# Two transformer stacks on one core: who stores the experts' blocks, and in which order the work between the last two layers is issued

## Chip, core and metric

The program runs on one core of one Trainium2 chip. The core has five engines with queues of their own: PE (TensorE, matrix products), DVE (VectorE), ACT (ScalarE), POOL (GpSimd) and SP (SyncE, which here only issues transfers). They meet through semaphores: an instruction raises one, a wait on another engine holds that engine's queue until it has the value. The metric is the time of one execution on the device in microseconds, lower is better.

## What is computed

A first stack of two layers over 256 tokens (feed-forward, mixer, feed-forward, gated side input), then a second stack of two layers over the same 256 tokens and 256 tokens of context. The change lies in the second stack, in the first of its layers' mixture of experts and in the start of its second layer:

```python
for i in range(DEPTH):                       # DEPTH = 2
    h  = _modulate(_rmsnorm(x,  norm1_g[i]), sh1,  sc1)
    hc = _modulate(_rmsnorm(xc, norm1_g[i]), shc1, scc1)
    y, yc = mixer(h, hc)                     # layer 1: queries from h, keys and values from h and hc
    x = x + g1 * y                           # and xc alike, in layer 0
    h2 = _modulate(_rmsnorm(x, norm2_g[i]), sh2, sc2)
    f = _hier_moe(tokens, ...)               # tokens: h2, in layer 0 with the context's behind it
    x = x + g2 * f[:s]                       # and xc alike, in layer 0
return _rmsnorm(x, final_g)

def _hier_moe(t, ...):                       # 32 experts, two for each token
    xb = t_pad[buf_tok].reshape(n_blk, MOE_BLOCK, d)     # tokens sorted by expert, in blocks
    yb = (silu(x_blk @ w_gate[e]) * (x_blk @ w_up[e])) @ w_down[e]
    out.at[buf_tok].add(yb * buf_w)          # each token: its two experts' rows, weighted
```

## The kernel before

**Layout.** All activations of the second stack lie in SBUF (one tensor, `arena`), features on the 128 partitions: `k.x` is 8 feature tiles by 512 tokens, tokens 0 to 255 being x and 256 to 511 the context. Four token tiles of 128 follow from this: t = 0 and 1 are x's, t = 2 and 3 the context's. Products go to PSUM (`ps`). Everything is float32.

**Experts of layer 0** (`pe_experts_picked` and its counterparts, lines 2254 to 2360). A block is 32 assigned rows of one expert. How many blocks an expert has is known on the chip alone, so each engine runs, for each of 32 experts, a loop whose bounds it reads from SBUF (`first_block`). For a block, PE makes gate and up (line 2274, 64 products of 128 columns by four row groups, 128 records in the trace), picks the next block's rows (line 2249), turns the hidden values (line 2281) and the next rows (line 2575) and makes down (line 2289). ACT applies silu (line 2304) and copies the next block's rows out (line 2306). DVE makes the hidden product (line 2343), copies both turned tiles (2346, 2325) and prepares the pick of the block after (2237 to 2243). The down product of 32 rows lies on the partitions as four groups of 32, each with a quarter of the 1024 columns; ACT copies it to a ring of two places, `yring` (line 2309).

**Stores.** ACT stores too. In the loop over block g, `act_store_rows` (lines 2313 to 2319) stands between the copy of line 2306 and that of line 2309: it waits for the copy of block g - 1 and **for the stores of block g - 2 to have landed** (semaphore `y_out`), and then issues four transfers of 32 rows by 256 columns with the result of block g - 1 into the DRAM tensor `expert_out`. After the last expert it is called once more for the last block.

**Weights.** SP loads 6 MB an expert as three transfers of 2 MB (line 1890), into ten places of 2 MB, nine of them used here. The loads of expert e are issued once expert e - 3 has ended (`moe_ended`, raised by line 2292). PE waits for gate and up before an expert's loop, for down in the first block.

**Between the layers.** When the last expert has ended, GpSimd waits for all stores, raises `pool_ended` (line 2357) and issues eight indirect gathers of 512 KB (line 2360), two for each of the four token tiles. For each tile ACT scales one gathered tile (2368), DVE adds the other (2377), PE turns eight 128 by 128 squares (2395), DVE adds them to `k.x` (2383). When all four tiles are done, ACT squares the eight feature tiles of all 512 tokens (1376), PE sums them with a matrix of ones (1369), ACT takes the root (1385), DVE the reciprocal (1403), then DVE and ACT make the normed tiles, 8 features by two streams (1408, 1390). PE makes eight query tiles q1 of x (line 1443, eight products each, 16 records in the trace) and after each the rotation of the one before (1425), then the keys (k1) of both streams. In ACT's queue six small loads for layer 1 stand behind the normed tiles (`b_sink`, router weights, a table of constants). SP loads the second layer's query, key and value weights in four chunks (8 to 11) once experts 30 and 31 have ended, and the output weights (12 and 13) right behind.

**Layer 1** has its own experts' stage, with the results added in PSUM and no stores. Its weights come through ten places of 2 MB, each reloaded when its last reader has ended.

## Time and profile before

| | us |
|---|---|
| median of 3 runs | 3054.65 |
| lowest and highest run | 3050.98 and 3055.48 |
| profiled execution | 3052.24 |
| its span, first to last instruction | 3050.9 |
| PE busy (share of the span) | 2681.6 (88%) |
| DVE, ACT, GpSimd busy | 750.2, 481.6, 103.3 |
| experts of layer 0, first product to last result | 1799.6 to 2305.4 |
| from there to the first query product | to 2360.2 |
| query tiles, to the first key product | to 2394.3 |

A profile is of one execution, and its times of single steps are to be set against that execution's 3052.24 us. A row of a timeline gives start and duration and, in brackets, how long the engine stood idle before it and what ended the wait. DMA shares are means over 16 transfer engines; above 0.99 they have no gap. PEclk 1.00 stands for 2.4 GHz and 0.50 for 1.2 GHz.

### The profile page before, as it was taken

To read this page: it belongs to the slowest core of one execution; us is meant where nothing else is said; L and a number is where in the kernel's file an instruction comes from. 1 tells how busy PE (TensorE), PEld (TensorE's weight loads), DVE (VectorE), ACT (ScalarE), POOL (GpSimd) and SP (SyncE) were. 2 spreads that over 40 slices of the span, in tenths; PEclk is the share of its full clock that TensorE was granted. 3 is DMA by queue.
4 is the path that set the end of the run, shared out by engine and by line. 5 is a ranking of instruction groups with operands and counts; after the bars stand their busy time and mean duration, and the time that the engine had idled before them with its cause. 6 is when DMAs were issued, how large, how long until landed. Compare 5 with 4: busy or idle time off the path is not lost.

```text
span 3050.9 us, 57138 instructions
## 1 busy us (share of the span) xinstructions
PE 2681.6 (88%) x24486; PEld 1990.2 (65%) x24486; DVE 750.2 (25%) x2036; ACT 481.6 (16%) x1179; POOL 103.3 (3%) x144
## 2 busy tenths in 40 slices
PE   8999999999999999997997888887774998777766
PEld 7888688887888788884444556665552566554444
DVE  2002520023002520013117421111113153332223
ACT  2001310011001310012006320110002052000001
POOL 1001010011001010010000000000001000000000
PEclk9999999999999999998999999999986999999999
DMA  7544474546553466535210049899996114999997
GB/s 263 184 161 129 144 253 166 180 142 214 165 181 111 161 235 202 186 112 189 85 56 28 31 182 414 346 362 420 421 420 225 60 56 173 405 419 419 420 419 309
DMA packets 254651, 689.99 MB, mean 226 GB/s; under 512 B 15119, under 2 KB 148958, under 8 KB 238046
## 3 DMA queue, kind: packets, MB, share of 16 engines
q1 hardware_dynamic: 237696, 674.96, 58.6%
q10 hardware_dynamic: 15582, 7.61, 0.9%
q8 instruction: 173, 2.83, 0.4%
q0 software_dynamic: 1152, 4.19, 0.3%
q14 instruction: 48, 0.39, 0.0%
HBM read 669.95 MB, written 16.78 MB: 225 GB/s over the span
## 4 chain that ended last, share of the span: by engine, by line
PE 69%; DMA 17%; DVE 6%; issue 3%; ACT 3%; ACTq 2%; POOL 0%; SPq 0%; DVEq 0%
PE ps L663 18%; PE ps L674 10%; DMA arena<-in_moe_w_up 10%; DMA expert_out<-arena 7%; PE ps L1443 6%; PE ps L2607 3%; PE ps L1489 2%; PE ps L894 2%; PE ps L687 2%; PE ps L2274 2%; PE ps L1054 2%; PE ps L2030 2%; ACTq L2319 2%; PE ps L2568 1%; PE ps L2631 1%
## 5 line engine op out<-in xcount | busy, mean ns | idle before, releaser
L663 PE MATMUL ps<-arena 128*128 128x256 f32 x2560 | 568.6, 379 | 3.5 <-DVE arena L745 3.5
L663 PEld LDWEIGHTS ps<-arena 128*128 128x128 f32 x2560 | 483.0, 189 | 73.8 <-issue 4.1
L674 PE MATMUL ps<-arena 128*128 128x256 f32 x1408 | 318.0, 379 | 0.0
L674 PEld LDWEIGHTS ps<-arena 128*128 128x128 f32 x1408 | 264.9, 189 | 46.2 <-issue 8.4
L2274 PE MATMUL ps<-arena 128*32 128x128 f32 x6016 | 192.9, 286 | 55.3 <-issue 53.4
L2274 PEld LDWEIGHTS ps<-arena 128*32 128x32 f32 x6016 | 178.3, 115 | 64.2 <-issue 60.4
L2607 PE MATMUL ps<-arena 128*32 128x128 f32 x4096 | 139.8, 295 | 74.7 <-issue 72.9
L1443 PE MATMUL ps<-arena 128*128 128x512 f32 (+2 forms) x512 | 192.8, 548 | 11.3 <-ACT arena L1390 11.2
L787 DVE TENSOR_TENSOR arena<-arena,ps 128x256 f32<-128x256 f32 x76 | 32.1, 422 | 638.4 <-ACT arena L755 633.8
L2607 PEld LDWEIGHTS ps<-arena 128*32 128x32 f32 x4096 | 126.2, 119 | 82.6 <-issue 81.7
L1443 PEld LDWEIGHTS ps<-arena 128*128 128x128 f32 (+1 forms) x512 | 89.5, 180 | 104.7 <-issue 97.4
L755 ACT ACTIVATE arena<-ps 128x256 f32<-128x256 f32 x76 | 29.2, 384 | 675.1 <-PE ps L663 675.1
L2249 PE MATMUL ps<-arena 128*32 128x256 f32 x1536 | 102.4, 397 | 9.8 <-issue 6.8
L2289 PE MATMUL ps<-arena 128*32 128x256 f32 x1504 | 100.5, 406 | 4.1 <-issue 3.8
L2343 DVE TENSOR_TENSOR arena<-arena,ps 128x128 f32<-128x128 f32 x47 | 13.5, 288 | 360.0 <-ACT arena L2304 360.0
L2631 PE MATMUL ps<-arena 128*32 128x256 f32 x1024 | 63.8, 388 | 35.6 <-DVE arena L2719 35.6
L2249 PEld LDWEIGHTS ps<-arena 128*32 128x32 f32 x1536 | 58.9, 114 | 35.2 <-issue 11.8
L532 POOL TENSOR_TENSOR arena<-arena 128x256 f32<-128x256 f32 x64 | 42.8, 670 | 1081.4 <-DVE arena L500 1072.9
L894 PE MATMUL ps<-arena 128*128 128x256 f32 x352 | 77.4, 379 | 0.0
L2289 PEld LDWEIGHTS ps<-arena 128*32 128x32 f32 x1504 | 50.6, 114 | 38.1 <-issue 17.0
L2568 PE MATMUL ps<-arena 128*32 128x256 f32 x528 | 68.4, 638 | 8.0 <-issue 4.7
L894 PEld LDWEIGHTS ps<-arena 128*128 128x128 f32 x352 | 66.3, 189 | 9.5
(441 smaller groups left out, 2988.3 us busy)
## 6 DMA issues: line engine op xcount, KB each, us to landing
arena<-in_moe_w_gate SPq DMA_DIRECT2D x64, 2048.0 KB, 23.0
arena<-in_moe_w_up SPq DMA_DIRECT2D x64, 2048.0 KB, 24.7
arena<-in_moe_w_down SPq DMA_DIRECT2D x64, 2048.0 KB, 29.5
arena<-in_mod_w SPq DMA_DIRECT2D x24, 2048.0 KB, 13.2
arena<-in_w_gate SPq DMA_DIRECT2D x44, 1024.0 KB, 5.5
arena<-in_w_up SPq DMA_DIRECT2D x44, 1024.0 KB, 8.1
arena<-in_w_down SPq DMA_DIRECT2D x44, 1024.0 KB, 4.9
arena<-in_w_in SPq DMA_DIRECT2D x12, 1024.0 KB, 6.0
```

What stands on the lines that cost most here:

```text
L663: last = pe.matmul(k.ps[:, T % 4, off:off + S], w[:, t, T % 2 * P:(T % 2 + 1) * P], h[:, t, :], start=(t == 0), stop=(t == KT - 1), skip_g ...
L674: last = pe.matmul(acc[:, t, :], d[:, T % 2, t * P:(t + 1) * P], k.hid[:, T % 4, :], start=(T == 0 and t % 2 == 0), stop=end, skip_group_c ...
L687: last = pe.matmul(k.ps[:, T, off:off + S], w[:, t, T * P:(T + 1) * P], k.hu[:, t, :], start=(t == 0 and off == 0), stop=(t == KT - 1), sk ...
L894: last = pe.matmul(dst, w[:, t, j * P:(j + 1) * P], src[:, t, :], start=(t == 0), stop=(t == KT - 1), skip_group_check=True)
L1054: last = pe.matmul(k.banks(4, 4, S)[:, j, :], w[:, t, (j % 2) * P:(j % 2 + 1) * P], k.y[:, t, :], start=(t == 0), stop=(t == KT - 1), skip ...
L1443: last = pe.matmul(k.ps[o:o + m, j % 4, 0:ntok], w[:, t, c0:c0 + m], k.h2[:, t, 0:ntok], start=(t == 0), stop=(t == KT - 1), tile_position ...
L2249: last = k.nc.tensor.matmul(k.ps[32 * q:32 * q + 32, 1, 0:256], m.pick[:, t, :], m.rows[:, t, 256 * q:256 * q + 256], start=(t == 0), stop ...
L2274: last = pe.matmul(ps[BL * q:BL * q + BL, 0, a:a + F], m.xeT[:, t, :], wv[:, t, F * q:F * q + F], start=(t == 0), stop=(t == KT - 1), tile ...
L2289: last = pe.matmul(ps[BL * q:BL * q + BL, 3, 0:W], m.hT[:, f, :], wd[:, f, W * q:W * q + W], start=(f == 0), stop=(f == 3), tile_position= ...
L2568: last = k.nc.tensor.matmul(k.ps[32 * q:32 * q + 32, bank, 0:256], m.pick[:, t, :], rows, start=(t == 0), stop=(t == 1), tile_position=(0, ...
L2607: last = pe.matmul(ps[BL * q:BL * q + BL, 0, a:a + F], m.xeT[:, t, :], wv[:, t, F * q:F * q + F], start=(t == 0), stop=(t == KT - 1), tile ...
L2631: last = pe.matmul(ps[BL * q:BL * q + BL, 3, 0:W], m.hT[:, f, :], wd[:, f, W * q:W * q + W], start=(f == 0), stop=(f == 3), tile_position= ...
```

## The change

It has three parts.

1. GpSimd stores the blocks. ACT's four transfers a block are gone; `yring` has four places instead of two; ACT's copy of block g waits for `y_gone`, which GpSimd raises when it comes to a block whose parity's last stores have landed. GpSimd's loop takes two blocks a turn, one on semaphore `y_even`, one on `y_odd`. There are 47 blocks, so its last turn stores one place that holds no new block, and two pairs of stores ahead of the loop give both semaphores their first value. The gathers then wait for both.
2. Between the layers the two tiles of x are finished first, through norm and first query tile. The context's two tiles are combined, turned, added, summed and normed between the query tiles. The gathers land in `slots2[0]` and `Kflat`.
3. The six small loads of layer 1 are SP's. Chunk 11 waits for the gathers of tile 1, chunks 12 and 13 for the last turned context tile.

```diff
@@ act_experts_picked
             act.activation(m.xe, ps[:, 1, 0:256], ACT.Copy).then_inc(m.n["x_out"].sem, 1)
-            act_store_rows(k, m, g)
             act.wait_ge(*m.step("down", g, 1, 1))
-            act.activation(m.yring[:, bass.ds((g & 1) * W, W)], ps[:, 3, 0:W], ACT.Copy).then_inc(m.n["y_ready"].sem, 1)
-    act_store_rows(k, m, first_block(k, m, NE, ENG.Activation))
+            act.wait_ge(*m.step("y_gone", g, 0, 1))
+            act.activation(m.yring[:, bass.ds((g & 3) * W, W)], ps[:, 3, 0:W], ACT.Copy).then_inc(m.n["y_ready"].sem, 1)
+    act.activation(m.unread[:, 0:1], k.eps, ACT.Copy).then_inc(m.n["y_ready"].sem, 1)
@@ new, on GpSimd
+def pool_store_rows(k, m, g, b, which):
+    pool, BL, W = k.nc.gpsimd, m.BL, m.W
+    pool.wait_ge(*m.step("y_ready", b, 1, 1))
+    pool.wait_ge(which, g * STORE + STORE)
+    pool.wait_ge(m.n["y_gone"].sem, b + RING_AHEAD)
+    pool.tensor_tensor(m.unread[:, 1:2], m.unread[:, 2:3], m.unread[:, 2:3], ALU.add).then_inc(m.n["y_gone"].sem, 1)
+    pool_store(k, m, b, which)
+def pool_store(k, m, b, which):
+    for q in range(4):
+        k.nc.gpsimd.dma_start(k.ybuf[bass.ds(b * BL, BL), W * q:W * q + W], m.yring[BL * q:BL * q + BL, bass.ds((b & 3) * W, W)]).then_inc(which, 16)
@@ pool_experts
-    total = first_block(k, m, NE, ENG.Pool)
+    pairs = (first_block(k, m, NE, ENG.Pool) + 1) >> 1
+    pool_store(k, m, MAXROWS // m.BL + 2, even)
+    pool_store(k, m, MAXROWS // m.BL + 3, odd)
+    with pool.Fori(0, pairs) as g:
+        pool_store_rows(k, m, g, g * 2, even)
+        pool_store_rows(k, m, g, g * 2 + 1, odd)
+    pool.wait_ge(even, pairs * STORE + STORE)
+    pool.wait_ge(odd, pairs * STORE + STORE)
     pool.wait_ge(*s["moe_ended"].at(l, "expert", NE - 1))
-    pool.wait_ge(*m.step("y_out", total + 1, 0, 64))
@@ new, in place of pe_combine, pe_sums and pe_project for q1
+def pe_queries_between(k, m):
+    for t in range(2):
+        for g in range(2):
+            pe_turn_results(k, m, t, g, 2 * t + g)
+    for t in range(2):
+        for g in range(2):
+            pe_sum_part(k, t, g, 6 + t)
+    for j in range(KT):
...
+        last.then_inc(*s["pr_tile"].up("q1", j))
+        if j > 0:
+            pe_rotate_queries(k, j - 1)
+        if j == 1:
+            pe_turn_results(k, m, 2, 0, 6)
+            pe_turn_results(k, m, 2, 1, 7)
+        if j == 2:
+            for g in range(2):
+                pe.wait_ge(*s["moe_added"].at(0, 2, g))
+                pe_turn_results(k, m, 3, g, 6 + g)
+        if j == 4:
+            pe.wait_ge(*s["moe_added"].at(0, 3, 1))
+            for t in (2, 3):
+                for g in range(2):
+                    pe_sum_part(k, t, g, 4 + t)
+    pe_rotate_queries(k, KT - 1)
+def act_queries_between(k, m):
...
+    for j in range(KT):
+        act_project_tile(k, "q1", k.Q, S, j)
+        if j == 2:
+            for t in (2, 3):
+                for g in range(2):
+                    act_square_part(k, m, t, g)
...
+        if j >= 6:
+            for t in range(3 * j - 16, 3 * j - 13):
+                act_shift_stream(k, t, 1)
+def dve_queries_between(k, m):
...
+    dve_weigh(k, m, 0)
+    dve_weigh(k, m, 1)
+    for t in range(2):
+        for g in range(2):
+            dve_add_results(k, m, t, g, 2 * t + g)
...
+    for t in range(KT):
+        dve_norm_stream(k, t, 0)
+    dve_weigh(k, m, 2)
+    dve_weigh(k, m, 3)
+    for j in range(KT):
+        dve_project_tile(k, "q1", k.Q, S, j)
+        if j < 2:
+            for g in range(2):
+                dve_add_results(k, m, 2 + j, g, 6 + g)
...
+        if j >= 6:
+            for t in range(3 * j - 16, 3 * j - 13):
+                dve_norm_stream(k, t, 1)
@@ sp_program
-    sp_chunk(k, 11, 5, columns(w, D + S, S), s["moe_ended"].at(0, "expert", 31))
+    sp_chunk(k, 11, 5, columns(w, D + S, S), s["gathered1"].at(0, 1))
     w = a["b_w_o_2"][0]
-    sp_chunk(k, 12, 0, columns(w, 0))
+    sp_chunk(k, 12, 0, columns(w, 0), s["moe_turned"].at(0, 3, 1))
     sp_chunk(k, 13, 1, columns(w, 512))
+    sp.dma_start(k.sink, a["b_sink_2"].broadcast_to([P, 16])).then_inc(*s["sink_in"].up())
+    router_load(k, sp, ms[1])
+    sp.dma_start(*ms[1].const3).then_inc(*s["const31"].up(1))
```

The parts named in the new functions are the old steps cut by token tile: `act_weigh` and `dve_weigh` combine one tile of 128 tokens, `pe_turn_results` turns four squares, `dve_add_results` adds four, `act_square_part` and `pe_sum_part` take four feature tiles of 128 tokens, `act_root_part` and `dve_factor_part` the factors of 128 tokens, `dve_norm_stream` and `act_shift_stream` one normed feature tile of one stream.

**ACT, one block of the last expert's loop.** Before, with the stores from line 2317 on (ISA rows compute registers and addresses or wait):

```order
L2304 ACTIVATE arena<-ps 128x128
L2305 REGISTER_ALU
L2306 ACTIVATE arena<-ps 128x256
L2317 ISA
L2319 ISA
L2319 REGISTER_ALU
L2319 ISA
L2319 DMA expert_out<-arena 32x256
```

After, the same place:

```order
L2317 ACTIVATE arena<-ps 128x128
L2318 REGISTER_ALU
L2319 ACTIVATE arena<-ps 128x256
L2322 REGISTER_ALU
L2322 ISA
L2322 ACTIVATE arena<-ps 128x256
```

The four transfers (one is shown of the four) have left the place between the rows' copy and the result's.

**GpSimd, from the block counts to the gathers.** Before there was nothing between the counts and the gathers' release; after, this is half a turn of the loop, ahead of the same gathers:

```order
L2360 ISA
L2362 TENSOR_TENSOR arena<-arena 128x1
L2369 ISA
L2369 REGISTER_ALU
L2369 ISA
L2369 DMA expert_out<-arena 32x256
L2369 ISA
L2369 DMA expert_out<-arena 32x256
```

Four such transfers a block now stand in GpSimd's queue, eight in a turn.

**PE, from the last expert to the keys.** Before:

```order
L2395 MATMUL ps<-arena 128x128 x32
L1369 MATMUL ps<-arena 128x512 x8
L1443 MATMUL ps<-arena 128x256 x16
L1425 MATMUL ps<-arena 128x256
L1443 MATMUL ps<-arena 128x256 x8
```

After (2414 turns, 2439 sums, 2488 is a query tile, 2512 a rotation):

```order
L2414 MATMUL ps<-arena 128x128 x16
L2439 MATMUL ps<-arena 128x128 x16
L2488 MATMUL ps<-arena 128x256 x16
L2512 MATMUL ps<-arena 128x256
L2414 MATMUL ps<-arena 128x128 x8
L2488 MATMUL ps<-arena 128x256 x8
L2512 MATMUL ps<-arena 128x256
L2414 MATMUL ps<-arena 128x128 x8
L2488 MATMUL ps<-arena 128x256 x8
L2512 MATMUL ps<-arena 128x256
L2488 MATMUL ps<-arena 128x256 x8
L2512 MATMUL ps<-arena 128x256
```

Half of the turns and sums moved behind the first query tiles; the other 16 sums stand behind the fifth tile.

## Rows read from the trace of the kernel before

**Rows 1.** the page, groups: line, engine, operation, count | busy, mean | idle

```profile
L2343 DVE TENSOR_TENSOR arena<-arena,ps 128x128 f32<-128x128 f32 x47 | 13.5, 288 | 360.0 <-ACT arena L2304 360.0
```

**Rows 2.** the page, the chain that ended last, shares of the span by line

```profile
PE ps L663 18%; PE ps L674 10%; DMA arena<-in_moe_w_up 10%; DMA expert_out<-arena 7%; PE ps L1443 6%; PE ps L2607 3%; PE ps L1489 2%; PE ps L894 2%; PE ps L687 2%; PE ps L2274 2%; PE ps L1054 2%; PE ps L2030 2%; ACTq L2319 2%; PE ps L2568 1%; PE ps L2631 1%
```

**Rows 3.** busy time by stretch, two stretches of the experts (us)

```profile
core 0: us, PE busy (x) PEld busy (x) DVE busy (x) ACT busy (x) POOL busy (x), PEclk, DMA share, GB/s
1826.00:2095.00 269.00, 225.89 (x5285) 171.75 (x5279) 45.31 (x162) 26.48 (x80) 0.00 (x0) 0.96 0.95 381
2095.00:2292.00 197.00, 143.64 (x3134) 105.91 (x3122) 27.50 (x96) 17.13 (x49) 0.00 (x0) 0.91 1.01 419
```

**Rows 4.** order of time, an unhindered block: start us, us, engine, line

```profile
1807.92 3.67 PE L2274 MATMUL ps<-arena 128*32 128x128 f32 x128
...
1816.23 3.70 PE L2274 MATMUL ps<-arena 128*32 128x128 f32 x128
```

**Rows 5.** order of time, a block whose results had to wait for a store

```profile
1858.82 1.88 ACTq L2319 DMA_DIRECT2D expert_out<-arena  x4
...
1858.85 0.70 PE L2274 MATMUL ps<-arena 128*32 128x128 f32 x10 [2.88 <-issue]
...
1860.91 0.38 ACT L2309 ACTIVATE arena<-ps 128x256 f32 x1 [11.32 <-issue]
1862.05 0.28 ACT L2304 ACTIVATE arena<-ps 128x128 f32<-128x128 f32 x1 [0.76 <-issue]
```

**Rows 6.** groups by line, 1834 to 2095 us: busy, mean | idle, releaser

```profile
L2309 ACT ACTIVATE arena<-ps 128x256 f32 x26 | 10.0, 384 | 200.3 <-issue 185.2 <-DMA expert_out<-arena 12.6 <-PE ps L2289 2.6
...
L2281 PE MATMUL ps<-arena 128*128 128x128 f32 x26 | 8.6, 329 | 26.6 <-DVE arena L2343 26.6
```

**Rows 7.** chain in order of time, two up weights: start us, us

```profile
2094.94 25.77 DMA arena<-in_moe_w_up
...
2260.33 31.82 DMA arena<-in_moe_w_up
```

**Rows 8.** transfers issued between 1816.5 and 1817.0 us: size, us to landing

```profile
arena<-in_moe_w_up SPq DMA_DIRECT2D x1, 2048.0 KB, 13.4
```

**Rows 9.** line 2319, the stores: duration ns min/median/max, and landing

```profile
L2319 ACTq DMA_DIRECT2D expert_out<-arena x192: 327/328/1583, 1805.4 to 2311.1; - x192
...
DMA to landing us min/median/max: 1.5/5.9/11.2
```

**Rows 10.** order of time, the last block's results and first gather

```profile
2305.02 0.38 ACT L2309 ACTIVATE arena<-ps 128x256 f32 x1 [2.81 <-PE ps L2289]
...
2309.47 1.98 ACTq L2319 DMA_DIRECT2D expert_out<-arena  x4
...
2316.62 1.12 POOL L2360 DMA_INDIRECT arena<-expert_out,arena  x1 [0.17 <-issue]
```

**Rows 11.** line 2360, the gathers: duration ns, first and last start us

```profile
L2360 POOL DMA_INDIRECT arena<-expert_out,arena x8: 933/937/1124, 2316.6 to 2325.5; - x8
```

**Rows 12.** order of time, from the combination to the query tiles

```profile
2329.95 1.15 ACT L2368 ACTIVATE arena<-arena 128x1024 f32<-128x1024 f32 x1 [2.88 <-DMA arena<-expert_out,arena]
...
2332.47 1.97 PE L2395 MATMUL ps<-arena 128*128 128x128 f32 x8 [1.99 <-DVE arena L2377]
...
2344.39 10.19 PE L1369 MATMUL ps<-arena 128*128 128x512 f32 x16 [2.83 <-ACT arena L1376]
...
2355.20 3.37 DVE L1403 RECIPROCAL arena<-arena 128x256 f32<-128x256 f32 x2 [11.24 <-ACT arena L1385]
...
2360.17 9.66 PE L1443 MATMUL ps<-arena 128*128 128x256 f32 x32 [5.58 <-ACT arena L1390]
...
2373.99 3.62 PE L1443 MATMUL ps<-arena 128*128 128x256 f32 x16
...
2394.26 6.29 PE L1443 MATMUL ps<-arena 128*64 128x512 f32 x16
```

**Rows 13.** granted clock (PEclk) between the layers, columns as rows 3

```profile
2310.00:2350.00 40.00, 13.48 (x39) 8.78 (x40) 13.57 (x38) 9.61 (x13) 7.87 (x9) 0.50 0.60 227
```

239 lines of the change are left out of this document (149 added, 90 removed).

## Prediction

> **What bounds the kernel now.** The page comes first. Its chain by line gives 7% of the span to the transfer `expert_out<-arena` and 2% more to the issue of line 2319 [rows 2], and this is a result going out to memory, which nobody should have to wait for. 7% of 3050.9 us are 214 us, but that is no price: the chain only names the queue it passed. So I read next what the experts of layer 0 are short of, by stretches [rows 3]. From 2095 to 2292 us the transfer engines have no gap, at 419 GB/s: weights bound the stage there, and nothing that engines do quicker helps. From 1826 to 2095 us they moved 381 GB/s, so the equivalent of (1 - 381/419) x 269 = **24.4 us of transfer time was not used**. PE isn't full either, 226 of 269 us. Something else holds both.
>
> The timeline names it. Unhindered, one block follows another after 1816.23 - 1807.92 = 8.31 us [rows 4]. In a later block gate and up are made by about 1859.6, but silu starts at 1862.05, because ACT stands behind its own queue: the four stores could only be issued at 1858.82, when the ones before had landed, then came the result's copy at 1860.91, then silu [rows 5]. A store takes up to 11.2 us to land, 5.9 in the median [rows 9], more than a block. Grouped from 1834 to 2095 us, PE stood idle 26.6 us before line 2281, released by DVE's hidden product, which waits for silu [rows 6]. These 26.6 us of PE and the 24.4 us of transfers are the same loss seen from two sides, since weights are asked for only when PE has ended an expert. Silu's lateness is what the first part of the change removes.
>
> Between the layers it is a chain through all engines: results stored, gathered, combined, squared, summed, normed, and PE mostly idle at the lower clock [rows 10, 12, 13].
>
> **Part 1, stores on GpSimd, in the experts.** Each of the 47 blocks has four issues on ACT in the loop, and four more follow it, 192 in all [rows 1, 9]. They leave the way of silu. The new wait of ACT, `y_gone`, holds silu too, but asks only that GpSimd has come to block g - 2, for which the stores of block g - 4 must have landed. What GpSimd needs for a block: the trace has no plain transfer issued by it. The nearest row from above is its indirect gather, 0.94 us and one every (2325.5 - 2316.6) / 7 = 1.27 us [rows 11]; from below ACT's store, 0.33 us for one [rows 9]. Taking GpSimd's own row, a block costs 4 x 1.27 + 0.2 + waits, about 5.5 us, hidden behind PE's 8.3. With 11.2 us to land [rows 9], one parity turns in 5.5 + 11.2 = 16.7 us for two blocks, 8.35 a block, just PE's pace and well under the stage's mean of (2305.4 - 1799.6) / 47 = 10.8 us. So I take the stores at nothing inside the stage.
>
> The gain is then bounded by the weights. The up weights of experts 20 and 31 landed at 2094.94 + 25.77 = 2120.7 and 2260.33 + 31.82 = 2292.15 [rows 7]: eleven experts in 171.4 us, **15.6 us an expert** at full rate, the stores' bytes included. Those of expert 3 landed at 1816.6 + 13.4 = 1830.0 [rows 8]. 28 experts at full rate would take 436.4 us instead of 462.2, so at most 25.8 us can be had. Not all of it: where experts with two blocks follow one another PE needs 16.6 us an expert, one more than the weights, and a load waits for the end of the expert three back, so the queue runs dry now and then. I take off 4 us. **-22 us**, between -10 (stalls of PE's own in the stretch, which the transfers would otherwise have hidden, take over) and -26.
>
> **Part 1, the tail.** The last result is ready at 2305.40 and the first gather starts at 2316.62, 11.2 us later, since ACT issued the last stores only at 2309.47 [rows 10]. After the change GpSimd issues at once, but also the place without a block: 8 transfers. At 1.27 us the last starts 0.5 + 4 x 1.27 + 0.3 + 3 x 1.27 = 9.7 us after the result; it lands 4 us later (the last of ACT's took 5 beside weights, the quickest of all 1.5 [rows 9]); 0.4 us for the raise. 14.1 instead of 11.2, **+3 us**. At 0.5 us an issue it would be 8.7 us, so the range is -2.5 to +5. I stay with GpSimd's own row.
>
> **Parts 2 and 3, gathers.** Tile 1 is weighed from 2329.95, 13.3 us after the first gather started [rows 10, 12]. 4 MB of output weights went through at the same time: they were issued behind chunk 11, and now wait until the context is turned. Four gathers are 2 MB, 5 us at 419 GB/s, the fourth issued after 3.8 us: 9 us. **-4.3 us**, 0 to -5.
>
> **To the first query product.** Before, from 2329.95 to 2360.17 are 30.2 us. After, from the same event: scale 1.15 and add 1.28, turning (half of 1.97 for four squares [rows 12]), DVE's adds for two tiles, 16 of 0.27, squares 0.63; PE's 16 small sums, 32 records of 128 columns. The turns' 8 records of that width took 1.97 us, 0.25 each at the lower clock, and the old sums' 16 records of 512 columns 10.19 us, 0.64 each [rows 12], so 2 us for each four sums (1.3 by columns alone), and the last two fours end after the last add. Root 0.4, reciprocal of 128 columns 3.37 / 4 = 0.85 [rows 12], first norm and shift 0.8. In order: PE is through the turns 4.6 us after the event and through the sums at 11.5, first product at 13.5. If the clock rises earlier 11.5, if every handing over costs more 18. It stays low as long as PE is idle as before: 0.50 from 2310 to 2350 [rows 13]. **-16.7 us**, -12 to -19.
>
> **Through the query tiles.** Before 2394.26 - 2360.17 = 34.1 us [rows 12]. The first two tiles took 9.66 us as both streams were being normed; a tile alone takes 3.62, so 2.7 us go. PE now does 16 turns (2.2 us at the full clock, half of 1.97 for eight) and 16 sums (4 to 8 by the same rows, I take 5) between the tiles. And a new wait: ACT's copy of tile 7, on which the last rotation hangs, is queued behind three shifts of the context, which wait for DVE's norms, which are queued behind tile 6's rotation. PE stands some 2.9 us there (sine and add 0.85, three norms 1.25, shift 0.4, copy 0.4). -2.7 + 2.2 + 5 + 2.9 = **+7 us**, +4 to +12. What was moved beside other work costs nothing: six small loads leave ACT's queue, where they stood after the norm with PE busy, and on SP stand ahead of layer 1's weights, whose places come free later anyway. From the keys on nothing changes, and layer 1 shifts as a whole, as its weights are asked for by its own readers.
>
> **Sum.** -22 + 3 - 4.3 - 16.7 + 7 = -33.0 us. 3052.24 - 33 = 3019.2 for the profiled execution; the median of the runs is 2.4 us above it, so **3021 us**.
>
> **Rivals.** (a) *PE's own stalls replace the stores'.* Even when nothing waited for a store PE sometimes stood inside gate and up; if such stalls keep the transfers from filling up, the experts give 10 us instead of 22: 3033 us. For it: at 419 GB/s PEclk is 0.91 only [rows 3]. Against: PE has 32 x 15.6 - 47 x 8.31 = 109 us in hand over the stage. (b) *The context's work stays on the way*: waits between query tiles, by turned tiles or DVE's queue, cost 10 us more: 3031 us. (c) *GpSimd becomes the bound*, the case on the other side. It decides at (10.8 - 0.5) / 4 = 2.6 us for one issue. At 3.1 us a block costs 12.9, and 47 of them 606 us instead of 506: 100 us lost, 14 more in the tail, whose eight issues take 25 us instead of 10, and the 14 won between the layers against it: about 3155 us. Against it: 0.94 us for the gather of four times the rows [rows 11], and DVE is busy 45 of 269 us only [rows 3], in pieces of 0.29 us [rows 1].
>
> The Trainium skill, page "SBUF — State Buffer", section "SBUF: two separate sides", has a rule that would bring (c) about: descriptors for GpSimd's transfers can't be written while VectorE holds the port pair that both share, and one took 3.1 us beside a copy instead of 0.62. By 3.1 us throughout it would be (c); by 0.62 the tail would be shorter. No row of this trace has such a transfer, so it bears on the chance alone.
>
> (d) *The queue keeps full and the tail is short*: -26, -2.5 and the rest as above, 3012 us.
>
> **Chances.** The forecast 0.56, (a) 0.17, (b) 0.10, (d) 0.07, (c) 0.10. The range 3012 to 3040 leaves out (c) and little else. A measurement of this kernel tells 0.2%, 6 us, from no change. Faster 0.90, since all cases but (c) are at least 14 us below; of (c) 0.02 may end within 6 us, just past its point of 2.6 us; slower 0.08.
>
> **What would show it.** In the profile after: transfers above 410 GB/s from 1826 us on; no idle before the transpose of the hidden values to speak of; the last result near 2283 us; GpSimd's issues about 1.2 us apart; the first query product some 37 us after the last result and not 55; the keys 41 us behind it; from there to the end the same 656.6 us. Wrong would be: ACT waiting long at the result's copy, or layer 1 taking back what was won.

## The result, and the profile after

The changed kernel takes **3017.77 us** (median of 4 runs, 3016.83 to 3024.55), the kernel before 3052.82 us beside it (median of 4, 3049.05 to 3055.48). The ratio is 0.9895, with a 95% interval from 0.9879 to 0.9910: about one per cent faster, clear of the noise, by 35 us where 32 to 34 were forecast. The profiled execution took 3016.83 us; its span is 3015.6 us.

The page of the kernel after, the groups that answer to the stores and to silu's readers (columns as in [rows 1]), and the same stretches as [rows 3] by engine busy time, clock and transfers:

```profile
L2287 PE MATMUL ps<-arena 128*32 128x128 f32 x6016 | 193.6, 286 | 61.1 <-issue 58.6
...
L2369 POOL DMA_DIRECT2D expert_out<-arena x200 | 100.3, 502 | 69.8 <-issue 30.9
...
L2347 DVE TENSOR_TENSOR arena<-arena,ps 128x128 f32<-128x128 f32 x47 | 13.5, 288 | 310.6 <-ACT arena L2317 310.6
```

```profile
core 0: us, PE busy (x) PEld busy (x) DVE busy (x) ACT busy (x) POOL busy (x), PEclk, DMA share, GB/s
1826.00:2095.00 269.00, 238.02 (x5632) 174.21 (x5625) 49.63 (x174) 29.98 (x86) 63.22 (x144) 0.98 1.01 415
2095.00:2280.00 185.00, 137.74 (x2928) 103.32 (x2918) 24.30 (x86) 15.32 (x44) 32.85 (x75) 0.88 1.01 417
```

From 1826 us on the transfers have no gap now: 415 GB/s where [rows 3] has 381, and PE does 238 us of work in 269 instead of 226. What the engines wait for, grouped by line, first PE and DVE from 1834 to 2095 us (answers to [rows 6]), then ACT over the whole stage:

```profile
L2294 PE MATMUL ps<-arena 128*128 128x128 f32 x28 | 9.4, 335 | 0.0
```

```profile
L2322 ACT ACTIVATE arena<-ps 128x256 f32 x47 | 18.1, 385 | 126.1 <-PE ps L2302 126.1
...
L2317 ACT ACTIVATE arena<-ps 128x128 f32<-128x128 f32 x47 | 13.1, 278 | 230.3 <-PE ps L2287 230.3
```

Before the turn of the hidden values PE had stood idle 26.6 us [rows 6]; now it is 0.0. ACT waits for products alone, never for a store and never for GpSimd. The last result, in order of time with GpSimd's stores and gathers behind it (start us, us; answers to [rows 10, 11]):

```profile
2283.45 0.39 ACT L2322 ACTIVATE arena<-ps 128x256 f32 x1 [2.59 <-PE ps L2302]
...
2284.86 2.38 POOL L2369 DMA_DIRECT2D expert_out<-arena  x4 [0.59 <-issue]
2287.26 0.20 POOL L2362 TENSOR_TENSOR arena<-arena 128x1 f32<-128x1 f32 x1
2287.74 2.39 POOL L2369 DMA_DIRECT2D expert_out<-arena  x4 [0.27 <-issue]
2291.66 0.19 POOL L2387 TENSOR_TENSOR arena<-arena 128x1 f32<-128x1 f32 x1 [1.53 <-DMA expert_out<-arena]
...
2292.47 1.02 POOL L2390 DMA_INDIRECT arena<-expert_out,arena  x1 [0.62 <-issue]
```

The result is there 21.6 us sooner than before, and the first gather follows 8.6 us behind it, not 11.2. PE between the layers, down to the first key product (answers to [rows 12]):

```profile
2301.71 1.97 PE L2414 MATMUL ps<-arena 128*128 128x128 f32 x8 [18.48 <-DVE arena L2406]
2305.23 1.97 PE L2414 MATMUL ps<-arena 128*128 128x128 f32 x8 [1.55 <-DVE arena L2406]
2306.99 5.04 PE L2439 MATMUL ps<-arena 128*128 128x128 f32 x32
2314.63 7.15 PE L2488 MATMUL ps<-arena 128*128 128x256 f32 x32 [2.60 <-ACT arena L2461]
...
2322.05 1.04 PE L2414 MATMUL ps<-arena 128*128 128x128 f32 x8
...
2335.47 3.73 PE L2439 MATMUL ps<-arena 128*128 128x128 f32 x32
...
2353.92 1.21 PE L2512 MATMUL ps<-arena 128*128 128x256 f32 x2 [3.05 <-ACT arena L1463]
```

Read from such rows of each kernel's profiled execution, one term after the other (us; each column counts from the one to its left):

| | last result | first gather | tile 1 weighed | first query product | first key product | from there to the end |
|---|---|---|---|---|---|---|
| before | 2305.4 | +11.2 | +13.3 | +30.2 | +34.1 | +656.6 |
| after | 2283.8 | +8.6 | +10.2 | +11.9 | +40.4 | +660.5 |
| difference | -21.6 | -2.6 | -3.1 | -18.3 | +6.3 | +3.9 |
| forecast | -22 | +3 | -4.3 | -16.7 | +7 | 0 |

The sum is -35.4 us, the difference of the spans -35.3. So the size came out, while one term had the wrong sign and one was overlooked: layer 1 took 3.9 us back. Part of the closeness is luck, since the tail (first gather behind the last result) was 5.6 us better than forecast and this made up for the 3.9 us.

### The profile page after: what moved, and what is told of

Its sections match the earlier page's. It is cut to its first block, busy times and chain, and to the rows that moved or that the text cites. A ratio compares the mean times of both kernels' runs of the same rounds, so it can differ in the third digit from the quotient of the medians.

```text
span 3015.6 us, 57462 instructions
## 1 busy us (share of the span) xinstructions
PE 2670.6 (89%) x24534; PEld 1982.5 (66%) x24534; DVE 751.3 (25%) x2039; ACT 483.6 (16%) x1182; POOL 212.8 (7%) x392
## 4 chain that ended last, share of the span: by engine, by line
PE 76%; DMA 12%; DVE 5%; issue 3%; ACT 3%; SPq 0%; ACTq 0%; POOL 0%; POOLq 0%; DVEq 0%
PE ps L663 18%; DMA arena<-in_moe_w_up 11%; PE ps L674 10%; PE ps L1443 5%; PE ps L2287 5%; PE ps L2262 3%; PE ps L2790 3%; PE ps L2302 3%; PE ps L1497 2%; PE ps L894 2%; PE ps L687 2%; PE ps L1054 2%; PE ps L2042 2%; PE ps L2751 1%; PE ps L2814 1%
## 5 line engine op out<-in xcount | busy, mean ns | idle before, releaser
L2287 PEld LDWEIGHTS ps<-arena 128*32 128x32 f32 x6016 | 177.6, 115 | 71.9 <-issue 67.6
L2790 PEld LDWEIGHTS ps<-arena 128*32 128x32 f32 x4096 | 125.5, 118 | 90.0 <-issue 89.0
L1443 PE MATMUL ps<-arena 128*128 128x512 f32 (+1 forms) x384 | 162.6, 601 | 5.6 <-ACT arena L1390 5.6
L1443 PEld LDWEIGHTS ps<-arena 128*128 128x128 f32 (+1 forms) x384 | 64.6, 174 | 94.7 <-issue 91.7
L2369 POOL DMA_DIRECT2D expert_out<-arena x200 | 100.3, 502 | 69.8 <-issue 30.9
L2347 DVE TENSOR_TENSOR arena<-arena,ps 128x128 f32<-128x128 f32 x47 | 13.5, 288 | 310.6 <-ACT arena L2317 310.6
L2262 PEld LDWEIGHTS ps<-arena 128*32 128x32 f32 x1536 | 57.4, 112 | 37.8 <-issue 14.0
```

The costliest lines, as they stand in the source:

```text
L1443: last = pe.matmul(k.ps[o:o + m, j % 4, 0:ntok], w[:, t, c0:c0 + m], k.h2[:, t, 0:ntok], start=(t == 0), stop=(t == KT - 1), tile_position ...
L2262: last = k.nc.tensor.matmul(k.ps[32 * q:32 * q + 32, 1, 0:256], m.pick[:, t, :], m.rows[:, t, 256 * q:256 * q + 256], start=(t == 0), stop ...
L2287: last = pe.matmul(ps[BL * q:BL * q + BL, 0, a:a + F], m.xeT[:, t, :], wv[:, t, F * q:F * q + F], start=(t == 0), stop=(t == KT - 1), tile ...
L2369: k.nc.gpsimd.dma_start(k.ybuf[bass.ds(b * BL, BL), W * q:W * q + W], m.yring[BL * q:BL * q + BL, bass.ds((b & 3) * W, W)]).then_inc(which ...
L2790: last = pe.matmul(ps[BL * q:BL * q + BL, 0, a:a + F], m.xeT[:, t, :], wv[:, t, F * q:F * q + F], start=(t == 0), stop=(t == KT - 1), tile ...
```

## The experiments

Each kernel below is timed beside the kernel before on the same chip; "the stage" is the time from the landing of expert 3's up weights to the landing of expert 31's, which leaves out what happens ahead of both. It is 462.1 us in before and 440.9 in after. Where no range is given, the time is that of one execution.

### Each part alone

The stores on GpSimd, with everything between the layers as before:

```diff
@@ the kernel before
-            act_store_rows(k, m, g)
+            act.wait_ge(*m.step("y_gone", g, 0, 1))
@@ pool_experts, pool_store_rows and pool_store as in the change
```

> The kernel before with part 1 alone: GpSimd stores the blocks, everything between the layers as before. Theory 1 (the two parts add up, each worth what the traces of before and after differ by in its stretch): the last result 21.6 us earlier, near 2283.8, the first gather 2.6 us sooner behind it (8.6 instead of 11.2 us), nothing between the layers, so 24.2 us less than before, a ratio of 0.992. Rival (the stretches interact: an earlier end of the experts meets the weights of the next layer and is given back in layer 1): the last result as early, but the time only 20 us or less below before, with the loss in the stretch from the first key product to the end, which was 656.6 us before and 660.5 us after.

Measured: 3030.86 us (3025.73 to 3034.19) against 3050.87, ratio 0.9939 [0.9923, 0.9956]. Stage 440.1 us, 415 GB/s from 1826 to 2095 us. The experts gained what was expected, but the whole gained 20.0 us and not 24.2: the first gather comes 11.7 us behind the last result, where 8.6 were expected. From the first gather on every term is before's within 0.1 us, except for the first query product (29.3 instead of 30.2): 656.7 us from the first key product to the end. So nothing was given back in layer 1; what is missing is the tail.

The order between the layers as in the change, ACT's stores as before:

```diff
@@ the changed kernel
-            act.wait_ge(*m.step("y_gone", g, 0, 1))
+            act_store_rows(k, m, g)
```

> The kernel before with parts 2 and 3 alone: ACT stores as before, x's tiles finished first. Theory 1 (additive): the last result at 2305.4 as before, the first gather 11.2 us behind it, then 10.2 us to the second tile's weighing instead of 13.3, 11.9 us to the first query product instead of 30.2, 40.4 us of query tiles instead of 34.1, 1.1 us lost in the key tiles: 14.0 us less than before, a ratio of 0.9954. Rival (interaction): the ACT queue with its last stores delays the first weighing, and less than 10 us is left.

Measured: 3036.31 us (3034.05 to 3040.15), ratio 0.9953 [0.9936, 0.9969]. The stage is 458.0 us, and the same stretch as [rows 3] reads as in before:

```profile
1826.00:2095.00 269.00, 226.78 (x5289) 170.48 (x5281) 45.52 (x162) 26.69 (x80) 0.00 (x0) 0.96 0.95 386
```

First query product 12.2 us behind tile 1, first key product 40.2 behind that, and 665.4 us from there to the end; layer 1's attention took 145.0 us of these, at the lower clock for a stretch in it, where after has 140.4 and the kernel with the tail's stores left out 144.1. The two parts alone save 20.0 and 14.6 us, 34.6 together, and both at once 35: in total they add up. And what layer 1 takes back, it takes back in the kernel with the second part alone.

The tail's gain, though, doesn't belong to GpSimd. With the new order and ACT's stores the first gather comes 8.0 us behind the last result, as soon as with GpSimd's (8.6); with GpSimd's stores and the old order it comes after 11.7, no sooner than in before (11.2). What the new order changes there is the traffic: chunks 11 to 13 of the weights were issued 0.7 us ahead of the last result to 3.9 us behind it, and now are held back. From the last result to the first gather, first with the stores alone, then in after (columns as [rows 3]):

```profile
2279.60:2291.20 11.60, 0.00 (x0) 0.00 (x0) 0.00 (x0) 0.03 (x1) 4.58 (x11) 0.60 0.98 331
2284.00:2292.40 8.40, 0.00 (x0) 0.00 (x0) 0.24 (x2) 1.43 (x2) 4.58 (x11) 0.60 0.39 126
```

GpSimd's last store starts 5.8 us behind the last result in both; it lands 4.9 us later in the first and 1.9 us later in the second.

### Was it ACT's waiting, or the bytes, or two blocks at once?

The stores of one block only once those of the block before have landed:

```diff
     with pool.Fori(0, pairs) as g:
+        pool.wait_ge(odd, g * STORE + STORE)
         pool_store_rows(k, m, g, g * 2, even)
+        pool.wait_ge(even, g * STORE + 2 * STORE)
         pool_store_rows(k, m, g, g * 2 + 1, odd)
```

> The kernel after, GpSimd waiting before each block's stores for those of the block before, not of the one before that: the two semaphores no longer overlap. Theory 1 (what cost time was that ACT did the waiting in front of silu): 2.4 us of issue and 5.8 in the median to land are 8.2 us a block, up to 11.4, under the mean of 10.3 and with two places of slack, so the last result stays within 2 us of 2283.8. Rival (the overlap of two blocks' stores is what helped): the last result moves back towards 2305, by 10 us or more.

Measured: 3020.14 us against 3053.63, stage 441.5, last result at 2283.25, where after has 2283.84. The first gather comes 12.1 us behind it, 3.5 later than in after, because the empty place's stores now stand behind the landing of the last real ones. Inside the stage the overlap of two blocks is worth nothing; it was enough that silu no longer stood behind the stores. The ring of results has four places here as in after, and no kernel was run in which ACT goes on issuing from a ring of four, with more time for a store to land. So that ACT's waiting was the cost is shown; that it takes a second engine to remove it isn't.

The kernel before with no stores in the loop (only the last block's):

```diff
             act.activation(m.xe, ps[:, 1, 0:256], ACT.Copy).then_inc(m.n["x_out"].sem, 1)
-            act_store_rows(k, m, g)
@@ act_store_rows
-    act.wait_ge(*m.step("y_out", g, 0, 64))
@@ pool_experts
-    pool.wait_ge(*m.step("y_out", total + 1, 0, 64))
+    pool.wait_ge(*m.step("y_out", 1, 0, 64))
```

> The kernel before with the blocks' stores left out of ACT's loop (the one after the loop stays; the experts' results then never reach the gathers, so the output isn't the reference's). Theory 1 (in after stores cost the stage only their bytes): the last result at 2283.8 less the 47 x 0.13 MB at 419 GB/s that aren't moved, 14.7 us of transfer time, of which the stage's full queue gives back all: 2269 to 2272. Rival (PE and the fetch of its instructions are the limit by now, not the weights): within 4 us of 2283.8.

Measured: 3020.30 us against 3053.63, stage 432.1, 8.7 us less than in after. The last result comes at 2276.3, between the two theories. The bytes of 47 blocks, 6.2 MB, are 14.7 us at 419 GB/s, and only 8.7 of them come back: from 1826 to 2095 us the transfers go at 406 GB/s here (415 in after), so without the stores something else holds them a little. So of the 30.0 us that the stores cost the stage before, 21 were ACT's waiting, which the change removed, and 9 remain. As 9 are less than the bytes alone would take, nothing points to a wait that is left.

### How far is GpSimd from being the bound?

Eight issues for a block, each half the rows, and sixteen, each a quarter (the counts that the semaphores are waited for grow with them):

```diff
     for q in range(4):
-        k.nc.gpsimd.dma_start(k.ybuf[bass.ds(b * BL, BL), ...], m.yring[BL * q:BL * q + BL, ...])
+        for r in range(0, BL, 16):          # 8 in the second kernel
+            k.nc.gpsimd.dma_start(k.ybuf[bass.ds(b * BL + r, 16), ...], m.yring[BL * q + r:BL * q + r + 16, ...])
```

> The kernel after, each block stored by eight transfers of 16 rows instead of four of 32. An issue on GpSimd took 0.60 us from one to the next in the trace of after (four in 2.4 us), so a block costs GpSimd 4.8 + 0.8 us. Theory 1 (GpSimd is the bound only from 10.8 us a block): the experts' stage ends as in after, last result near 2284, and only the tail grows by 8 x 0.6 = 4.8 us. Rival (what counts is how long a block's stores take from result to landing, 5.6 + 6 us for each parity of two blocks, near PE's 8.3): the last result 5 us later or more.

> The kernel after, each block stored by sixteen transfers of 8 rows. GpSimd then needs 16 x 0.6 + 0.8 = 10.4 us a block, the stage's mean in the kernel before being 10.8 and in after 10.3. Theory 1: GpSimd becomes the bound (rival c of the prediction at its point): about 47 x 10.4 = 489 us or a little more for the stage, last result at 2289 to 2300, ACT waiting at the result's copy for y_gone; the tail 32 x 0.6 = 19 us instead of 4.8. Rival (issues of smaller transfers are cheaper, in proportion to rows): 0.2 to 0.3 us each, and nothing changes.

Eight: 3021.75 us against 3053.63, stage 440.4, nothing lost in it; the tail grows to 13.6 us. Sixteen: 3073.38 us, stage 473.9, last result at 2317.7, later than the 2289 to 2300 expected, and a tail of 29.1 instead of some 23. GpSimd's stores and ACT's waits over the stage, of the kernel with sixteen (busy, mean, idle and its releaser):

```profile
L2370 POOL DMA_DIRECT2D expert_out<-arena x755 | 392.8, 521 | 114.3 <-issue 39.9
```

```profile
L2322 ACT ACTIVATE arena<-ps 128x256 f32 x47 | 18.1, 384 | 295.2 <-POOL arena L2362 253.2 <-PE ps L2302 42.0
```

GpSimd is busy or between two issues for (392.8 + 114.3) / 47 = 10.8 us a block, ACT waits 253 us for it, silu behind that, and the kernel is slower than before. The prediction's point for this rival was 10.8 us a block, four issues of 2.6 us, where the experts would end as late as in before. At 10.8 us they end 12.3 us later than in before, so the point lies a little lower; the changed kernel stays far from it because an issue takes 0.50 us.

### The tail

The empty place's stores left out, with one more loop that runs for an odd last block alone:

```diff
-    pairs = (first_block(k, m, NE, ENG.Pool) + 1) >> 1
+    total = first_block(k, m, NE, ENG.Pool)
+    pairs, single = total >> 1, total & 1
...
-    pool.wait_ge(even, pairs * STORE + STORE)
+    with pool.Fori(0, single):
+        pool_store_rows(k, m, pairs, pairs * 2, even)
+    pool.wait_ge(even, (pairs + single) * STORE + STORE)
```

> The kernel after, with the loop over pairs of blocks followed by one block only where the number is odd, so that the place without a block isn't stored (47 blocks: 188 transfers in the loops instead of 192). Theory 1 (the tail is GpSimd's eight issues): four issues and one small instruction fewer behind the last result, 2.9 us, so the first gather 5.7 us behind the last result instead of 8.6. Rival (the landing of the last real store sets it, 4 to 6 us after its issue at 2287): the tail gets shorter by under 1.5 us, since the four issues were hidden behind the landing.

Measured: 3020.91 us (3013.20 to 3022.93) against 3050.87, ratio 0.9897 [0.9877, 0.9918], no different from after. The end of the stage on GpSimd:

```profile
2285.01 2.38 POOL L2369 DMA_DIRECT2D expert_out<-arena  x4 [0.62 <-issue]
2291.55 0.19 POOL L2390 TENSOR_TENSOR arena<-arena 128x1 f32<-128x1 f32 x1 [4.16 <-DMA expert_out<-arena]
```

Where after waits 1.53 us for landings behind its eight issues, this one waits 4.16 us behind its four, and both gather 8.4 to 8.6 us after the last result. In after the last block's own stores have landed 7.0 us behind the result and the empty place's 7.7; without the empty place the own ones land after 7.4. So the two ends lie side by side, and taking the one away leaves the other.

### The wait ahead of the last rotation

ACT's copy of query tile 7 moved from behind the context's three shifts to ahead of them:

```diff
@@ act_queries_between
     for j in range(KT):
-        act_project_tile(k, "q1", k.Q, S, j)
+        if j < 7:
+            act_project_tile(k, "q1", k.Q, S, j)
...
+        if j == 6:
+            act_project_tile(k, "q1", k.Q, S, 7)
```

> The kernel after, with ACT's copy of query tile 7 moved ahead of the three shifts of the context in its queue, nothing else. In the trace of after PE stands 3.05 us before the last rotation, waiting for that copy. Theory 1: the wait goes, the first key product comes 2.7 to 3 us earlier, and the whole is 2.5 to 3 us below after. Rival: the key tiles start earlier but wait for the context's shifts instead, so that the first key product is earlier and the last one is not: 0 to 1 us.

Measured: 3014.94 us (3011.32 to 3015.89), ratio 0.9882 [0.9865, 0.9898]. In total this isn't told apart from after; in the trace it is. PE in order of time at the end of the query tiles:

```profile
2350.43 1.34 PE L2512 MATMUL ps<-arena 128*128 128x256 f32 x4
2351.69 16.73 PE L1443 MATMUL ps<-arena 128*64 128x512 f32 x48
```

The two last rotations run without a gap, and the first key product comes 36.9 us behind the first query product instead of 40.4. The key tiles take 49.5 us again, as before, where after takes 50.7. The granted clock in the first 5 us of the keys, after:

```profile
2355.00:2360.00 5.00, 5.00 (x10) 1.57 (x10) 2.04 (x5) 1.31 (x3) 0.00 (x0) 0.76 0.41 174
```

Behind PE's 3.05 us of standing still the clock was at its lower level for a moment, and 1.1 of the 3.9 us of layer 1 are that. So the wait cost 4.6 us, 3.5 of its own and 1.1 behind it.

### Chunks 9 and 10 behind the gathers

On top of tile 7's copy, the query weights' second chunk and the first key chunk wait for the gathers of tile 1, as chunk 11 does:

```diff
-    sp_chunk(k, 9, 3, columns(w, 512))
+    sp_chunk(k, 9, 3, columns(w, 512), s["gathered1"].at(0, 1))
     sp_chunk(k, 10, 4, columns(w, D, S))
-    sp_chunk(k, 11, 5, columns(w, D + S, S), s["gathered1"].at(0, 1))
+    sp_chunk(k, 11, 5, columns(w, D + S, S))
```

> The kernel a3 with the weight chunks 9 and 10 asked for only when the gathers of tile 1 have landed, as chunk 11 is. Theory 1 (weights in flight slow the last stores and the gathers): the first gather 7 us behind the last result instead of 8.4 to 9.7, the second tile weighed 9 us behind it instead of 10, 2 to 3 us less in all. Rival (chunk 9 then comes late for the fifth query tile, 16 us behind the first): a wait in front of it. Chunk 9 needs about 8 us from its issue, the tile comes some 24 us behind it, so I expect none.

Measured: 3012.46 us (3010.15 to 3016.03), ratio 0.9868 [0.9847, 0.9890]. The first gather comes 8.5 us behind the last result (9.7 in the kernel that it is built on), tile 1 is weighed 10.0 behind that (10.0), and the gathers still land in 6.2 us in the median instead of 6.4. For the gathers this was no test: in the kernel that it is built on the last of the chunks had landed 1.6 us before the first gather started, and in after 2 us before it, so there was no weight traffic beside them to take away. On the tail the chunks do bear: the last block's own stores land 4.6 us behind the result and not 7.7, and the 8.5 us are now the eight issues and the landing of the empty place. Leaving the empty place out would pay here; that kernel wasn't run.

### Where layer 1's other two microseconds went

In layer 1's experts before and after run alike up to the landing of the last weights: from the landing of the second reload to the last landing 431.0 and 430.7 us. But then the last gate and up products, for which all wait, took 3.7 us in before and 5.7 in after. PE in order of time, of before:

```profile
3030.08 3.71 PE L2607 MATMUL ps<-arena 128*32 128x128 f32 x128 [0.51 <-issue]
```

of after:

```profile
2992.79 4.43 PE L2790 MATMUL ps<-arena 128*32 128x128 f32 x103 [3.50 <-issue]
2997.52 0.95 PE L2790 MATMUL ps<-arena 128*32 128x128 f32 x25 [0.30 <-issue]
```

The one is a row of 128 records without a break; the other is broken behind record 103, with nothing that PE waits for. But the break itself is only 0.30 us. Most of the 2.0 us lie in the 103 records ahead of it, which ran at the lower clock:

```profile
2992.30:2995.60 3.30, 2.81 (x56) 2.69 (x60) 0.20 (x2) 0.00 (x0) 0.00 (x0) 0.50 0.46 185
```

PE had stood idle for 3.50 us ahead of this block, where in before it was 0.51 us and the clock stayed at 1.00. The kernel with tile 7's copy first has the same block at the full clock, and the break in it is longer:

```profile
2990.22 3.04 PE L2793 MATMUL ps<-arena 128*32 128x128 f32 x103 [2.11 <-issue]
2994.67 0.95 PE L2793 MATMUL ps<-arena 128*32 128x128 f32 x25 [1.41 <-issue]
```

That is 5.4 us in all, against 5.7: at either clock the records behind 103 begin 4.5 to 4.7 us into the block.

Such pauses, 0.3 to 3.4 us long, lie in many of the 32 blocks of layer 1, at the same records in the profiles of kernels with the same number of products ahead of them: in before, in the stores alone and in the kernel without stores in block 3 behind record 58, block 4 behind 107, block 6 behind 77, and so to 30 behind 101; in the kernels with the new order in block 2 behind 90, 4 behind 60, 5 behind 109, and so to 30 behind 54. Not every profile shows a pause at every place. Behind record 103 of block 31 five of the nine kernels with the new order have one; in the other four the clock was at 0.50 in this block, and it took 5.4 to 6.4 us without a pause of 0.3 us there. The new order of the work has 24 products more on PE (48 records). Block 31 is the last, for which everything waits, and there is nothing late in it before.

Three kernels tested whether the place follows from the number of products ahead. Each has one-column products more, which nobody reads, ahead of the query tiles, where PE waits anyway: 24 in the kernel before, 64 and 40 in the kernel with tile 7's copy first (the one with 40 has chunks 9 and 10 behind the gathers too).

```diff
@@ pe_combine of the kernel before (24), pe_queries_between (64, 40)
+    for _ in range(24):
+        pe.matmul(k.ps[0:32, 0, 511:512], k.c["ident"][:, 0:32], k.c["ident"][:, 0:1], start=True, stop=True, skip_group_check=True)
```

> The kernel before with 24 products of one column more on PE while it waits for the gathers, as many as the kernel after has more. Theory 1 (pauses move with the code): the pauses in layer 1 stand where after has them, 47 or 48 records earlier than in before, one of them after record 103 of the last expert's gate and up, which takes 5.4 us or more instead of 3.7; the stretch from the first gate product of layer 1 to the last expert's end 459 instead of 457.1 us. Rival: pauses as in before, 457 us.

> The kernel a3 (after with the copy of tile 7 first) with 64 products of one column more on PE, issued while it waits for the first gathers, so that they cost nothing themselves. In a3 as in after and in a2, PE pauses in the last expert's gate and up of layer 1 after the 103rd of its 128 records, 1.41 us with nothing in the profile that it waits for; in before, a1 and b4, whose PE program is before's, it has no pause there, but such pauses in other experts, always at the same records. Theory 1 (the pause belongs to a place in PE's program, where the next piece of code has to be fetched, and the place moves with the number of instructions ahead of it): all pauses move by 128 records, the last gate and up takes 3.7 us instead of 5.4, the time is 1.7 us below a3. Rival (it belongs to the moment, as the weights and the clock fall): the pause stays after record 103.

> The changed kernel with tile 7's copy out ahead of the shifts, chunks 9 and 10 of the query weights asked for behind tile 1's gathers, and 40 one-column products more ahead of the first query tile. 24 products more in the kernel before moved TensorE's pauses inside the gate and up products 47 or 48 records earlier, to where the changed kernel has them; 64 more left them where they were, and 64 products are 128 records. Theory 1, the pauses sit at places of the program that repeat every 128 records: 40 more than the changed kernel (64 more than before) puts them at before's places, within one record: block 3 at 59, 4 at 108, 6 at 78, 29 at 53, 30 at 102, and none late in block 31. The last gate and up products then take about 3.7 us and not 5.4, and the last expert ends about 11.8 us behind its up weights' landing and not 13.7: total about 3010.5 to 3013, 0.986 of before. Theory 2, 64 more left them alone because the products of the added kind don't count there and the 24 worked in another way: the places stay (30 at 54, 31 at 103), the last gate and up products take 5.4 us, total 3012.5 to 3015. Theory 3, the places move but the time they took is only taken elsewhere: last gate and up 3.7 us, but from the first key product to the end still 660 us. The 40 products run while TensorE waits for the rows of tile 1, and cost nothing ahead of the first query product.

24 more in before: 3055.24 us against 3052.13. The pauses are where after has them, one record off: block 2 behind 89, 4 behind 59, and so to 30 behind 53 and 31 behind 102. PE in the last gate and up, and in all that block 13.5 us from the landing of its up weights to the expert's end, where before takes 11.8:

```profile
3031.57 3.04 PE L2609 MATMUL ps<-arena 128*32 128x128 f32 x102 [1.85 <-issue]
3035.75 1.03 PE L2609 MATMUL ps<-arena 128*32 128x128 f32 x26 [1.14 <-issue]
```

64 more: 3012.52 us (3010.88 to 3014.28), ratio 0.9866 [0.9846, 0.9886]. The pauses did not move by a record, 31 behind 103 among them, and the last gate and up took 5.7 us. By the scale of the 24, whose 48 records moved the places by 47 or 48, 64 products are 128 records: so the places repeat at a distance of which 128 records are a multiple, and I had added one such distance. That gave the number for the last kernel, since 24 + 40 are 64 more than before.

40 more: 3012.54 us (3008.29 to 3017.52), ratio 0.9882 [0.9865, 0.9898]. The places are before's, one record off: block 3 behind 59, 4 behind 108, 6 behind 78, and so to 29 behind 53, 30 behind 102, and none late in 31. PE in the last block:

```profile
2986.26 3.71 PE L2795 MATMUL ps<-arena 128*32 128x128 f32 x128 [0.51 <-issue]
```

Its end comes 11.8 us behind the landing, as before. So the first theory holds for the places, and the second falls. In the total it isn't seen: from the first key product to the end this kernel still has 659.1 us, about what the third theory said. But what takes it is nothing that the pauses left behind. Two other things of the same size move from kernel to kernel. One is the clock at layer 1's first expert. In the kernel with 40 more (then in before):

```profile
2537.00:2544.00 7.00, 6.14 (x140) 5.38 (x144) 3.62 (x15) 0.28 (x1) 0.00 (x0) 0.70 0.02 4
```

```profile
2583.00:2590.00 7.00, 6.55 (x156) 4.51 (x160) 3.28 (x14) 0.45 (x2) 0.00 (x0) 1.00 0.01 4
```

At 0.70 in the mean the first expert took 12.1 us, at 1.00 it took 10.5; with 24 and with tile 7's copy alone it also took 12.2 and 12.3, with 64 10.5. Both times occur with either set of places, so they aren't the pauses' doing. The other lies ahead of the change: expert 3's up weights landed at 1826.1 to 1826.5 us in the stores alone, the kernel with eight issues and the one with 40 more, at 1828.7 in the one with one block's stores at a time, and at 1830.0 to 1831.6 in before, after and the others.

| | last result | first key product | key tiles | values to layer 1's experts | first expert of layer 1 | its last weights landed to its last expert's end | span |
|---|---|---|---|---|---|---|---|
| before | 2305.4 | 2394.3 | 49.5 | 139.7 | 10.5 | 11.8 | 3050.9 |
| after | 2283.8 | 2355.1 | 50.7 | 140.4 | 10.5 | 14.0 | 3015.6 |
| tile 7's copy first | 2283.3 | 2351.7 | 49.5 | 140.2 | 12.3 | 13.7 | 3012.8 |
| with 64 more | 2285.9 | 2354.3 | 49.5 | 139.7 | 10.5 | 14.0 | 3013.0 |
| with 40 more | 2281.3 | 2348.0 | 49.5 | 140.3 | 12.1 | 11.8 | 3007.1 |
| before with 24 more | 2303.8 | 2393.0 | 49.5 | 140.3 | 12.2 | 13.5 | 3053.9 |

What PE waits for in a pause can be read from the transfers. The trace has a queue of kind `instruction`, which moves packets of 16,384 bytes. The fourteen profiles have 166 pauses of 0.3 us or more inside layer 1's gate and up products, and each of them ends 1.2 to 1.6 us behind the end of such a packet. Around the 1.41 us pause above, in a window from 2992.0 to 2993.5 us, it is

```profile
q8 instruction: 1, 0.02, 4.4%
```

And counted in PE's instructions (products, weight loads and those of its sequencer), the distance from one pause to the next is a multiple of 256 in every one of the profiles. 24 products are 96 instructions, 48 of them records of products, which is the shift; 64 products are 256 instructions, which is why they bring all places back. So in a pause PE waits for the next piece of its program. Why a piece comes late isn't shown.

So of the 3.9 us that layer 1 took back in after, 2.2 lie in the last block, 1.1 are the clock behind PE's wait, and 0.7 lie between the values and the first expert, which I haven't followed. In the last block of after the lower clock and the late piece of program lie over each other and can't be told apart; before with 24 products more shows 1.7 us with the pause alone, at the full clock. The fastest kernels are those built on tile 7's copy, at 0.9866 to 0.9882 of before; with after at 0.9895 [0.9879, 0.9910] only their traces tell them from it.

## Why the prediction was right, point by point

**What the experts were short of: right.** The 24.4 us of unused transfer time and the 26.6 us of PE's idleness in front of the hidden values' turn [rows 3, 6] were one loss, and both went with ACT's stores: 415 GB/s, 0.0 us. The stores one at a time show that it was silu's place in ACT's queue and not the number of stores in flight. Forecast -22, measured -21.6; from expert 3 on 21.2 of the 25.8 us that full weight traffic allows [rows 7, 8]. The pace at full rate, 15.6 us an expert, is 15.6 again between experts 20 and 31.

**GpSimd's price: wrong, the term was mis-sized.** I took the indirect gather's own row, 0.94 us for one and 1.27 for the distance of two [rows 11], for a plain store. Measured are 0.50 us in the median and four in 2.38 us, so 0.60 apart. It changed nothing inside the stage, where even eight issues of 0.60, more than four of 1.27 would take, are hidden. In the tail it puts the last issue 5.8 us behind the result instead of 9.7. Between two rows of the trace, 0.33 for a store of ACT and 0.94 for GpSimd's gather of four times the rows, the price lay nearer to the same operation on another engine than to another operation on the same engine.

**The tail: wrong in sign, by two terms of which I named one.** Forecast were 9.7 us to the last issue, 4 to its landing and 0.4 for the raise, 14.1 in all and +3. Measured are 5.8, 1.9 and 0.9, so 8.6 and -2.6. The first is GpSimd's price. The second is the landing: the prediction counted the held-back chunks in the gathers' term alone and took the landing from stores beside weights. With the chunks in flight it was 4.9 us, and the tail 11.7 us, +0.5 on before. So GpSimd's stores by themselves gain nothing in the tail. The bound at half a microsecond gave 8.7 us, and 8.6 are measured, by luck: its issues are too quick and its landing too slow.

**Rival (c): held off, and its point nearly confirmed.** With sixteen issues GpSimd takes 10.8 us a block and is the bound: 3073 us, the experts 12.3 us later than in before. Behind it the Trainium skill, page "SBUF — State Buffer", section "SBUF: two separate sides", has descriptors wait while VectorE holds the shared ports, 3.1 us instead of 0.62. The trace of after doesn't show that case: its 200 issues are between 0.50 and 0.73 us long, with VectorE busy 50 of 269 us. This chance of one in ten rested on that rule more than on a row.

**The gathers: right in direction, 1.2 us too much.** I reckoned 5 us from the fourth gather's issue to its landing. Line 2390 in after, and ahead of it the first and the last start:

```profile
L2390 POOL DMA_INDIRECT arena<-expert_out,arena x8: 937/937/1195, 2292.5 to 2301.3; - x8
...
DMA to landing us min/median/max: 4.3/6.4/6.9
```

It took 6.4, and that with no weights beside it: the mis-sized term is the pace. From 2292.5 to 2302.7 us the transfers of after moved 249 GB/s, at a DMA share of 0.75, where the prediction reckoned with the weights' 419. That the output weights had been in the way is right: beside them the gathers took 7.2 to 10.8 us to land in before, and 4.5 to 6.7 in the kernel with the new order alone.

**To the first query product: right, 1.6 us too little.** PE is through the turns 4.5 us after the event (4.6) and through the sums at 9.3 (11.5), since the clock rose among them. The prediction had that as its lower end, 11.5 us to the first product; 11.9 are measured. The clock from the first turns on, after:

```profile
2302.00:2307.00 5.00, 3.45 (x17) 2.91 (x15) 3.11 (x9) 1.78 (x2) 0.46 (x1) 0.50 1.02 407
2307.00:2314.00 7.00, 5.03 (x33) 4.84 (x32) 4.76 (x13) 2.65 (x6) 0.00 (x0) 0.81 0.41 135
```

**Through the query tiles: right, step by step.** The first two tiles gave 9.66 - 7.15 = 2.5 us (2.7), the turns cost 2 x 1.04 = 2.1 (2.2), the sums 3.7 (5), and PE stood 3.05 us ahead of the rotation (2.9), released by ACT's copy in line 1463. This wait was found by asking what is queued behind the waiting instruction on its engine, and it could be taken away by one line.

**"From the keys on nothing changes": wrong by 3.9 us.** The step left out two things that pass through no semaphore: that the clock fell behind a wait of PE (3.05 us idle, then 0.51 from 2353.9 to 2357.4 us), and that 24 products more shift the places where PE waits for its program in a stage much later.

## What to carry to other kernels

An engine that has work for others in its queue shouldn't wait there for landings: the trace shows it as another engine's idleness, two steps away (PE before the turn of the hidden values), and the chain's share (7%) says nothing of its price (21 us). When the bytes are counted apart from the waiting, by a kernel without the stores, it is plain how much is left to win. Where a price isn't in the trace, look for the same operation on another engine as well as for another operation on the same one, and ask of the sum what changes its sign. And a term belongs to a part of the change only when that part alone shows it: the tail's gain looked like GpSimd's and was that of the held-back weights.

## What the runs showed of the hardware that was not expected

- A plain store issued by GpSimd takes 0.50 us of it for 32 rows of 256 values, 0.49 for 16 rows and 0.52 for 8, so its price is by the issue and not by the rows; it lands as ACT's do. Line 2369 in after (answers to [rows 9], where ACT's took 1.5, 5.9 and 11.2 us):

```profile
L2369 POOL DMA_DIRECT2D expert_out<-arena x200: 496/498/727, 1792.5 to 2289.6; - x100
...
DMA to landing us min/median/max: 1.7/5.8/9.0
```

- PE pauses 0.3 to 3.4 us inside long runs of products. The pauses lie a multiple of 256 of PE's instructions apart, and each of 166 ended 1.2 to 1.6 us behind a packet of 16,384 bytes on the queue of kind `instruction`. So the place of a pause is set by the number of PE's instructions ahead of it, and 64 products more (256 instructions) bring all places back. Over most of the stage the transfers were at 415 to 424 GB/s; whether that is why the pieces of program came late isn't shown.
- A pause costs nothing while weights are what is waited for: up to the last weights' landing before and after run alike, 431.0 and 430.7 us. In the last block it shows: from the last up weights' landing to the end 13.5 to 14.0 us instead of 11.8 in the table above, for a shift of 48 records.
